# The second layer's memory keys multiplied unsplit in the opening stage and kept in DRAM, in a two-block fp32 transformer kernel

## The reference, cut to what matters

```python
# first block: modulation of the normalised input by c
shift, scale, gate = split(silu(c) @ w_ada + b_ada, 3)
h = rms_norm(x, norm_g) * (1 + scale) + shift
a, b, c, d = split(h @ w_in)                  # four branches, of which d is computed first
...
# second block, layer i in (0, 1); layer 0 mixes by a convolution, layer 1 by differential attention
k_sh, v_sh = rms_norm(x, kv_norm) @ w_k_shared, rms_norm(x, kv_norm) @ w_v_shared   # layer 1
q = rms_norm(x, norm_mix[1]) @ diff_w_q
x = x + attention(q, k_sh, v_sh) @ diff_w_o
k = mem @ mem_w_k[i]                          # "memory keys": mem is an input, 256 x 1024
v = mem @ mem_w_v[i]
s = (rms_norm(x, norm_mem[i]) @ mem_w_q[i]) @ k.T
x = x + (softmax(s) @ v) @ mem_w_o[i]
x = x + (silu(h @ w_gate[i]) * (h @ w_up[i])) @ w_down[i]
```

## Time and profile before

| | us |
|---|---|
| three runs: median (lowest, highest) | 1110.13 (1109.71, 1111.43) |
| profiled execution: span from first to last instruction | 1111.3 |
| TensorE busy in it | 1092.0 (98%) |
| VectorE busy | 749.5 (67%) |
| ScalarE busy | 583.6 (53%) |
| DMA | 176 GB/s mean, 343 and 381 GB/s in the first two of 40 slices |

### The profile page before, as it was taken

One profiled execution on the slowest core, in us unless ns is written; L12 is line 12 of the kernel. 1 busy time (PEld: TensorE's weight loads), 2 busy tenths in 40 slices (PEclk: granted clock), 3 DMA queues, 4 the chain that ended last, 5 costly groups with the idle time before them and its releaser, 6 DMA issues.

```text
span 1111.3 us, 15418 instructions
## 1 busy us (share of the span) xinstructions
PE 1092.0 (98%) x6251; PEld 951.6 (86%) x6251; DVE 749.5 (67%) x1024; ACT 583.6 (53%) x940; POOL 54.4 (5%) x87
## 2 busy tenths in 40 slices
PE   8999999999999999999999999999999999999997
PEld 6799988788898988989988988788988989888986
DVE  5736776865679977555678855546967546788643
ACT  3458653444477775555444544456765545444442
POOL 3311000000010000001000000000011000000000
PEclk9999999999999999999999999999999999999999
DMA  9956464655654325535555555544445435555550
GB/s 343 381 161 207 135 196 162 233 184 189 223 168 126 115 77 189 175 99 149 197 184 184 196 182 196 189 153 151 152 153 189 132 115 190 190 190 189 162 179 38
DMA packets 118776, 195.09 MB, mean 176 GB/s; under 512 B 6586, under 2 KB 39762, under 8 KB 118705
## 3 DMA queue, kind: packets, MB, share of 16 engines
q1 hardware_dynamic: 116144, 187.51, 50.7%
q0 software_dynamic: 2560, 6.60, 2.0%
HBM read 193.04 MB, written 1.05 MB: 175 GB/s over the span
## 4 chain that ended last, share of the span: by engine, by line
PE 83%; DVE 10%; ACT 5%; issue 1%; DMA 1%; POOL 1%; SPq 0%; DVEq 0%; ACTq 0%; POOLq 0%
PE product L669 55%; PE small L706 5%; PE product L706 5%; DVE conv_out L2719 5%; PE product L708 3%; PE small L708 3%; PE product L996 3%; ACT w_high L591 1%; ACT diagonal L2612 1%; DVE w_low L601 1%; PE small L816 1%; PE small L2081 1%; PE small L731 1%; PE small L1462 1%; PE small L1451 1%
## 5 line engine op out<-in xcount | busy, mean ns | idle before, releaser
L601 DVE TENSOR_TENSOR w_low<-w_raw,w_high 128x2048 fp32r<-128x2048 f32 (+3 forms) x160 | 350.0, 2190 | 180.2 <-ACT w_high L591 178.6
L591 ACT ACTIVATE w_high<-w_raw 128x2048 fp32r<-128x2048 f32 (+3 forms) x160 | 292.1, 1832 | 175.9 <-PE product L669 144.2
L669 PE MATMUL product<-w_high,H 128*128 128x512 f32 (+2 forms) x736 | 239.7, 393 | 0.5 <-DVE w_low L601 0.5
L669 PEld LDWEIGHTS product<-w_high,H 128*128 128x128 f32 x736 | 137.9, 188 | 26.9 <-DVE w_low L601 0.9
L669 PE MATMUL product<-H,w_high 128*128 128x256 f32 x816 | 150.9, 283 | 0.1
L669 PE MATMUL product<-w_low,H 128*128 128x512 f32 (+2 forms) x368 | 142.3, 387 | 0.0
L669 PEld LDWEIGHTS product<-H,w_high 128*128 128x128 f32 x816 | 126.6, 188 | 1.1 <-DVE w_low L601 0.5
L669 PE MATMUL product<-H,w_low 128*128 128x256 f32 x408 | 114.2, 280 | 0.0
L706 PE MATMUL product<-H,w_high 128*128 128x512 f32 x256 | 89.1, 391 | 0.0
L706 PE MATMUL small<-H,w_high 128*128 128x512 f32 x256 | 89.1, 391 | 0.0
L669 PEld LDWEIGHTS product<-w_low,H 128*128 128x128 f32 x368 | 69.3, 188 | 11.9 <-issue 0.2
(11 more groups left out here) (412 smaller groups left out, 1784.3 us busy)
## 6 DMA issues: line engine op xcount, KB each, us to landing
w_raw<-in_ffn_w_gate SPq DMA_DIRECT2D x20, 1024.0 KB, 5.0
w_raw<-in_ffn_w_up SPq DMA_DIRECT2D x20, 1024.0 KB, 5.0
w_raw<-in_ffn_w_down SPq DMA_DIRECT2D x20, 1024.0 KB, 5.0
w_raw<-in_w_merge SPq DMA_DIRECT2D x16, 1024.0 KB, 5.2
w_raw<-in_w_ada SPq DMA_DIRECT2D x32, 256.0 KB, 6.5
w_raw<-in_mem_w_k SPq DMA_DIRECT2D x8, 1024.0 KB, 5.0
w_raw<-in_mem_w_v SPq DMA_DIRECT2D x8, 1024.0 KB, 5.0
w_raw<-in_conv_w_pw SPq DMA_DIRECT2D x16, 512.0 KB, 4.7
```

What stands on the lines that cost most here:

```text
L591: k.act.eng.activation(parts_of(k, i, j)[0], raw_of(k, i), ACT.Copy).then_inc(*k.act.tells("weights_high", ("weights high", i)))
L601: k.vec.eng.tensor_tensor(low, raw, high.bitcast(F32), ALU.subtract).then_inc(*k.vec.tells("weights_low", ("weights low", i)))
L669: mm = pe.eng.matmul(bank[:, off:off + wide], a, r, start=b not in started, stop=True, skip_group_check=True)
```

## The change

1. **Early keys.** mem_w_k of layer 1 is loaded in four chunks of 256 columns (1 MB each, `("early", n)`) through `w_raw`, and mem (1 MB) ahead of all else. PE turns mem and multiplies it with these chunks unsplit, 16 matmuls with 256 columns per chunk (`pe_early`): chunks 0 and 1 in front of the first quarter, 2 and 3 in front of the third and fourth. `pe_warm` goes except for three matmuls. ACT copies the products out, POOL writes them to DRAM (`kept_keys`), and reads them back at the start of the differential stage.
2. **X turned once.** The operand of w_q is made from the same turned banks as that of w_k and w_v, in a buffer of its own (`H_q`).
3. **Order of the attention stage.** w_k, then all of w_q, then the attention; its fill is w_v (four chunks), the memory values (four), the output projection.

```diff
+
+
+def early_chunk(w_k, n):
+
+    view = w_k.rearrange("(k p) n -> p k n", p=P)
+    return [(view[:, :, n * S:(n + 1) * S], S)], KT, ("early", n)
+
+
 def gate_modulation(ada, n):
...
     for q in range(QUARTERS):
-        plan.extend(first_modulation(ada, q) + first_weights(w_in, q))
+        halves = first_modulation(ada, q)
+        if q == 0:
+            plan.extend([early_chunk(later, 0), halves[0], early_chunk(later, 1), halves[1]])
+        else:
+            plan.extend(([early_chunk(later, q)] if q > 1 else []) + halves)
+        plan.extend(first_weights(w_in, q))
...
     feed(0)
     square(w["w_k_shared_2"])
-    square(w["w_v_shared_2"])
     even(w["diff_w_q_2"][0])
-    memory(1)
+    even(w["w_v_shared_2"])
+    even(w["mem_w_v_2"][1])
...
+def pe_early(k, n):
+
+    pe, i, key = k.pe, k.whole_weights["early", n], ("early", n)
+    raw, bank = raw_of(k, i), k.small.take(key)
+    pe.wait_ge(("weights", i), k.small.before(key))
+    for half in range(2):
+        for kt in range(KT):
+            if not n and not half and kt % CK == 0:
+                pe.wait_ge(("early whole", kt))
+            mm = pe.eng.matmul(bank[:, half * S:(half + 1) * S], raw[:, kt, half * P:(half + 1) * P], k.early_whole[:, kt, :], start=kt + half == 0,
+                               stop=True, skip_group_check=True)
+    mm.then_inc(*pe.tells("products", ("products", key), ("weights low", i)))
+
+
 def pe_condition(k):
...
-    pe_warm(k, 6)
+    for t in range(NT):
+        for g in range(0, KT, CK):
+            pe_early_turn(k, t, g)
+    pe_early(k, 0)
     pe.wait_ge("condition rows")
     tr(k.small.take("condition")[:, 0:3 * KT], k.cond_rows[:, :], k.ident[0:3 * KT, 0:3 * KT]).then_inc(*pe.tells("turned", "condition turned"))
-    pe_warm(k, 8)
+    pe_early(k, 1)
     pe_scale_and_turn_x(k)
-    pe_warm(k, 1)
     pe_first_columns(k, 0)
-    pe_warm(k, 3)
 
 
...
     for q in range(QUARTERS):
+        if q > 1:
+            pe_early(k, q)
...
+def act_early(k, n):
+    A, key = k.act, ("early", n)
+    A.wait_ge(("products", key))
+    A.eng.activation(k.early_out[:, 2 * n:2 * n + 2, :], k.small.of(key)[:, :].rearrange("p (k n) -> p k n", n=S), ACT.Copy).then_inc(
+        *A.tells("early_keys", "early keys", k.small.free(key)))
...
         act_first_quarter(k, q)
     A.ended("condition")
     act_split(k, QUARTERS)
     act_split(k, QUARTERS + 1)
+    act_early(k, 3)
     A.wait_ge(*k.all_ended("condition"))
...
-    g.wait_ge("d_v")
+    g.wait_ge("d_v", "early keys")
+    g.eng.dma_start(k.kept_keys, k.early_out[:, :, :]).then_inc(*k.landed("keep_keys", "keys kept"))
...
 def pool_differential(k):
+    k.pool.wait_ge("keys kept")
+    k.pool.eng.dma_start(k.mem_keys[:, :, :], k.kept_keys).then_inc(*k.landed("fetch_keys", ("mem keys", 1)))
...
+    def turn_queries(n):
+        for t in range(NT):
+            pe_turn_heads(k, "q heads", n, t)
+
+    def queries(n):
+        yield from pe_columns(k, ("w_q", n), k.H_q, KT, {(0, 15): lambda: turn_queries(0)} if n else {})
+
+    def values(n):
+        yield from pe_columns(k, ("w_v", n), k.H_kv, KT, {} if n else {(1, 4): lambda: turn_queries(1)})
+    for step in queries(0):
         if step == 0:
             for t in range(NT):
                 pe_turn_heads(k, "k heads", 1, t)
-
-    def turn_queries(n):
-        for t in range(NT):
-            pe_turn_heads(k, "q heads", n, t)
-
-    def queries(n):
-        yield from pe_columns(k, ("w_q", n), k.H_q, KT, {(0, 15): lambda: turn_queries(0)} if n else k.norms["q", 1].pe_behind(0, 1, (4, 8)))
+    drain(queries(1))
...
     def fill():
-        yield from queries(1)
-        yield from pe_memory_keys(k, 1, ({(0, 26): lambda: turn_queries(1)}, {}))
+        yield from values(0)
+        yield from values(1)
+        yield from pe_memory_keys(k, 1)
...
     filling = fill()
-    drain(queries(0))
-    next(filling)
-    pe.wait_ge(("k heads", 1), "diff values")
+    pe.wait_ge(("k heads", 1))
 
     def group(heads, t):
         nh, nk, key = len(heads), P * (t + 1), ("diff", heads[0], t)
...
-    sp.eng.dma_start(k.X[:, 0, :], x[:, 0, :]).then_inc(*k.landed("load_x0", ("x loaded", 0)))
+    early = w["mem_2"][0].rearrange("(t p) n -> p t n", p=P)
+    sp.eng.dma_start(k.early_rows[:, 0, :], early[:, 0, :]).then_inc(*k.landed("load_early0", ("early rows", 0)))
     sp.eng.dma_start(k.common[:, 0:COMMON_FIRST], w["common_constants"][:, 0:COMMON_FIRST]).then_inc(*k.landed("load_common", "common"))
     sp.eng.dma_start(k.c_row[:, :], w["c"][0].rearrange("(k p) -> k p", p=P)).then_inc(*k.landed("load_c", "c row"))
+    sp.eng.dma_start(k.early_rows[:, 1, :], early[:, 1, :]).then_inc(*k.landed("load_early1", ("early rows", 1)))
     values = None
...
             sp.wait_ge(("weights low", k.in_raw[n - k.N_RAW]) if n >= k.N_RAW else None)
+            if into == ("first", 0, 0):
+                sp.eng.dma_start(k.X[:, 0, :], x[:, 0, :]).then_inc(*k.landed("load_x0", ("x loaded", 0)))
```

More of the change, by code:

```diff
@@ L1019, in act_condition @@
     A.eng.activation(k.c_silu, k.small.of("c")[:, 0:KT], ACT.Silu).then_inc(*A.tells("c_silu", "c silu", k.small.free("c")))
+    for t in range(NT):
+        for g in range(0, KT, CK):
+            key = ("early row", g, t)
+            A.wait_ge(("turned", key))
+            A.eng.activation(k.early_whole[:, g:g + CK, t * P:(t + 1) * P], k.small.of(key)[:, :].rearrange("p (k n) -> p k n", n=P), ACT.Copy).then_inc(
+                *A.tells("early_whole", ("early whole", g), k.small.free(key)))
     sums = k.stat(("sums", "first"), NT)
@@ L2968, in group @@
         bank, p = k.small.take((key, "mixed")), k.turned.of(key)
-        pe.wait_ge(("turned rows", key), k.small.before((key, "mixed")))
+        pe.wait_ge(("turned rows", key), ("diff values", heads[0] // 4), k.small.before((key, "mixed")))
         for i, h in enumerate(heads):
@@ L3025, in rows_out, with values_out @@
             act_to_heads(k, "q heads", n, t, (("w_q", n), t), ("products", ("w_q", n)), ("k heads", "turned"))
+    def values_out(n):
+        for t in range(NT):
+            bank = (("w_v", n), t)
+            A.wait_ge(("root", "kv"), ("products", ("w_v", n)))
+            A.eng.activation(k.vals[:, t, n * CN:(n + 1) * CN], k.product.of(bank)[:, 0:CN], ACT.Copy, scale=k.norms["after", 0].root(t)).then_inc(
+                *A.tells("diff_values", ("diff values", n), k.product.free(bank)))
     told = {"groups": 0, "halves": 0}
     def fill():
+        rows_out(1)
         act_chunk(k)
-        turn_queries(0)
         yield
@@ L3040, in fill @@
         yield
[L3041 to L3042 removed]
+        values_out(1)
+        for n in range(D // CN):
             act_chunk(k)
@@ L3057, in act_differential @@
     act_chunk(k)
-    k.norms["q", 1].act_turn(1)
+    for t in range(NT):
+        act_turn_heads(k, "k heads", k.k_t, 1, t)
     act_chunk(k)
     rows_out(0)
+    act_chunk(k)
+    turn_queries(0)
+    act_chunk(k)
     filling = fill()
-    next(filling)
     scale = HD ** -0.5
```

113 lines of the change are left out of this document (63 added, 50 removed).

## The result

The changed kernel takes 1130.18 us (median of four runs, 1129.86 to 1131.93) against 1110.18 us before: ratio 1.0173 with a 95% interval of 1.0156 to 1.0190. It is slower, as forecast, but by 20.0 us and not by 11.5, and the time lies 2.7 us above the stated range.

The account below looks back on a forecast made before the run. TensorE, busy 98% of the span, was taken as the bound: opening +33.0, savings -25.8, attention +4.4 give +11.6 us on 1111.3, a span of 1122.9 and a median of 1121.7 us; range 1113.5 to 1127.5.

Parts of the forecast that it names:

- Start of the first quarter: Opening: loads, early chunks 0 and 1 and a low clock move the first quarter from 18.80 to 30.8 us, +12.0.
- Chunks 2 and 3: Opening, between the quarters: these early chunks lie in TensorE's full line and cost +14.1 us.
- The load held back: Third quarter: TensorE waits +3.6 us (bounds 0 to 5) because a w_ada load needs early chunk 2's buffer.
- The clock after such a wait: Behind the third quarter's wait: the clock falls, price 0 to 1.9 us, taken as +1.2.
- My cap of 1.9 us: Clock pricing: a low stretch lasts 3.7 us at most and wastes half of itself, so 0 to 1.9 us.
- The heads of branch d: c_q's start: its second load waits for early chunk 3's buffer, delaying the heads; TensorE waits +2.1 us (bounds 0 and 4).
- What goes away and the attention: Split keys, X's second turn and a gap save 25.8 us; waits before the projection's halves cost net +4.4.
- a sign of being wrong: Attention stage, w_k to the projection's end: shortening by less than 19 or more than 24 us would refute the prediction.
- its rule at hand one paragraph earlier: Clock rule from the kernel's end: the clock fell about 2.5 us after TensorE's work ended.
- From span to median: Whole kernel: the median of the runs is 1.2 us below the profiled span, so 1122.9 becomes 1121.7 us.
- the clock stays low: Rival: all of chunk 0 runs at 0.98 us per matmul and later waits cost 1.9 us each, 1129 us; 10%.
- transposes do not count for the clock as matmuls do: Opening: by the skill page mem's turns do not warm the array, making a low start of chunk 0 likelier.

Follow-up runs that it names:

- run without early matmuls: Changed kernel with 14 of the 16 matmuls of each early chunk left out, every load, turn and copy kept: 1116.41 us, ratio 1.0048.
- run with filled waits: Changed kernel plus matmuls nobody reads: 13 in the third quarter's wait, 7 and 5 before the output projection's halves: 1125.88 us, ratio 1.0129.
- kernels with and without early keys: Changed kernel with three edits combined, 1115.74 us, against the kernel without early keys with the heads' turn one step later, 1107.56 us.
- the first experiment: Changed kernel with the fourth early chunk multiplied inside the third quarter, before the column sums, instead of before the fourth quarter: 1118.96 us, ratio 1.0065.
- that with zeros at the start: Changed kernel with ten multiplications of zeros put back into the opening, around mem's turns and behind the first column sums: 1127.59 us, ratio 1.0146.
- the run with all edits: Changed kernel with fourth early chunk inside the third quarter, second chunk of w_q's second half in the attention's fill, zeros at the start: 1115.74 us, ratio 1.0038.
- the repeated unchanged run: The changed kernel measured once more, without further edits, beside the run with zeros: 1130.27 us, ratio 1.0168.

## Why the prediction was right and where it was wrong

Forecast on the span +11.6 us; the two profiled executions differ by 17.5, the medians by 20.0.

- **Start of the first quarter:** +12.0 forecast, +12.4 measured (31.23 against 18.80). The path is the forecast one: chunk 0 starts at its landing (10.7, forecast 11.0), and TensorE is never idle up to x's turn, so chunk 1's landing (17.8 to 18.3 us where TensorE waited for it in other profiles, not 19.2) plays no part here. The low clock cost 2.6 us (9.79 against 7.17), not 1.9. That the sum fits to 0.4 us is also luck of the execution: in four experiments with the same start, chunk 0 ran at the upper level and the first quarter started at 28.5 to 28.7, +9.7 to +9.9. The run without early matmuls splits it: 6.7 us come from the loads, the rest from TensorE. (In the opening the clock column reads 1.00 up to the first change on record, also where the first early chunk of the changed kernel runs at half pace; there the level is read from the pace of the matmuls.)
- **Chunks 2 and 3:** +14.1 forecast, 13.7 measured (6.8 for chunk 2; 6.9 for chunk 3, read where its clock was not low, in the run with filled waits): right.
- **The load held back:** place, cause and issue (54.7 forecast, 55.05 measured) right, **+3.6 was 5.6**. What failed is the time of the two loads, 5.0 + 2.7 us: the last of the eight pieces is issued 3.5 us after the first, at 58.54, and takes 5.8 us to land, so the two chunks are there 9.3 us after the first issue, at 64.3 and not 62.4. VectorE needs 1.8 us from there (its last four sums run from 62.97 to 66.15) and not 1.54. The 5.0 us came from a chunk loaded as one piece of 1 MB; these are pieces of 256 KB that SyncE issues 0.5 us apart. Sharing with c_q's chunk was excluded; what else slows them stays open.
- **The clock after such a wait:** **forecast +1.2, measured +3.9.** This is the step that failed most. My cap of 1.9 us came from the one place where the trace of before shows a low start (three matmuls, then the upper level), and I took its 3.7 us as the longest a low stretch lasts. Here it lasted 8 us of work: column sums +0.8, two 512-column matmuls +1.8, the fourth early chunk +1.3. Keeping TensorE busy through the wait took exactly this away. This execution is the dearest one: from the column sums to the fourth quarter it takes 13.46 us, and 9.62 with the wait filled; in the four other profiles with this wait and a whole chunk behind it, it is 11.96 to 13.17, a price of 2.3 to 3.6 us. All of them are above the cap.
- **The heads of branch d:** +2.1 forecast, +2.2 measured (c_q 8.75 us after the fourth quarter's start against 6.56).
- **What goes away and the attention:** -25.8 + 4.4 = -21.4 forecast. From the last turn of X before the attention (701.74 before, 738.15 after) to the last one in the kernel (924.6, 942.2) the stage shortens by 18.8, just under the 19 us that the prediction named as a sign of being wrong. The waits are 4.38 us against 4.6 forecast. The low clock behind the first, 1.6 us, **was priced at nothing**, though the prediction had its rule at hand one paragraph earlier. About 1 us more is missing, which no row of mine names; about as much is missing where the kernels with and without early keys were compared above.
- **From span to median:** forecast -1.2, and here the changed kernel's profiled run has a time of 1130.14 us for a span of 1128.8, 1.3 more, as every other run on record has. So the time that belongs to the span of before, 1111.3, is 1112.6 and not at most 1111.43: its profile was an execution 2.4 us slower than its median, which is what lies between the 17.5 and the 20.0. Windows of it:

```profile
188.00:192.00 4.00, 4.00 (x19) 3.66 (x19) 2.54 (x13) 0.26 (x1) 0.00 (x0) 0.63 1.05 403
192.00:196.00 4.00, 3.14 (x14) 2.17 (x13) 2.62 (x5) 0.78 (x3) 0.00 (x0) 0.94 0.09 36
```

A low clock in the branches, 1.5 us, stands in that profile, and not in the one of the changed kernel. Between c_q and the second block this alone brings the difference from 37.9 down to 36.5 us.

Added up: +4.8 in the opening (0.4, 2.0, 2.7, 0.1, less 0.4 for the chunks), +2.6 in the attention (1.6, and the 1.0 without a row), -1.5 for the low clock of before: 5.9 over the forecast 11.6, which is 17.5. The rival "the clock stays low" (1129 us, 10%) had the right price and the wrong place: it put the 5 us on the first early chunk and only 1.9 on each wait. Its own sum is off, too: 16 matmuls at 0.98 us are 15.7 us, 6.7 and not 5 more than the 8.9 taken, so it should have said about 1131 us.

The Trainium skill, "TensorE: Matmul & The Clock Gate", Part 1, says that the change of the clock depends on the phase at which the work meets the gate, so that equal kernels show different cold stretches. The runs agree that equal starts come out differently: the first early chunk takes 9.8, 9.8 and 9.1 us in three profiles and 7.2 in four others with the same start, and the wait of 2.5 us before the projection is followed by a low clock in the changed kernel and three others, but not in the first experiment and in that with zeros at the start. A rival stands for the first of the two: in the three slow ones mem's second half landed late and TensorE stood still for 0.8 to 1.6 us between its turns, in the four others for 0.4 us or not at all. Against that rival speaks the run without early matmuls: with a pause of 0.4 us too, it starts low (its first two early matmuls take 2.05 us). The prediction leant on Part 4 of the same page of the Trainium skill, that transposes do not count for the clock as matmuls do. The runs do not bear it out. In the first experiment nothing but a turn of c and mem's sixteen turns, at the lower pace (3.8 us for sixteen; in the run with all edits eight took 1.04), stands between 4.3 us and the first early chunk, which then runs at the upper level:

```profile
5.10 3.79 PE L750 MATMUL small<-common,early_rows 128*128 128x128 f32 x16
9.85 7.17 PE L1007 MATMUL small<-first_constants,w_raw 128*128 128x256 f32 x32 [0.95 <-DMA w_raw<-in_mem_w_k]
```

In the repeated unchanged run the clock does fall at 8 us, between the turns, but there TensorE had also waited 1.6 us. Zeros around the turns did not settle it either: with them the turns ran at the lower pace for eight of sixteen in one run and at the upper pace throughout in the other.

The direction was right and for the right reason: the early keys cost 24.6 us of TensorE's line at best and save 23.0 of split matmuls, before the waits that the shorter fill brings, and only the rest of the change is a gain.

## What to carry to other kernels

Work moved in front of a bound engine's stage is free only as far as the engine waited there; and the buffer it uses ties later loads to its place in that engine's order, so ask for each early chunk which load comes next into its buffer and who needs it. A wait of about 2 us or more on TensorE has to be priced with what follows it, up to 8 us of work at half clock here: put real work into it, or, where there is none, a few multiplications of anything. Take a change apart: here two of its three parts were worth 1.8 us as they stood and 3.4 with one turn a step later, hidden under a third that cost 21 to 23.

## What was not expected of the hardware

- After a wait of 5.6 us the clock stayed at 0.50 for nearly 8 us of TensorE work that was not dense (column sums, two 512-column matmuls, a third of a chunk), and for 4.7 to 7.3 us in five other profiles with that wait; after the wait of 2.5 us it was up again in about 4 us of dense matmuls.
- Even the wait of 1.80 us in front of the first quarter, behind turns and column sums, is followed by a low clock in four of the eight profiles that have it (the first quarter's first matmuls take 5.38 us in the first experiment, 3.69 in the changed kernel).
- Two loads of 1 MB in pieces of 256 KB into an empty queue: the first piece was used 3.5 us after the first issue, the fifth after 7.9 us, and holding back c_q's chunk behind them did not change the wait. DMA moved 217 GB/s from 55 to 60 us in the changed kernel and 364 from 60 to 65.
- The same opening starts its first quarter at 28.5 to 28.7 or at 30.7 to 31.2 us, by the clock at which TensorE meets its first chunk.
